# Four row groups at a time: low-rank pairs and head norms in the mixing stage of an RWKV-style block

## What is computed

```python
def token_shift_mix(z, mu):
    zp = jnp.pad(z, ((0, 0), (1, 1), (0, 0)))
    nb = 0.5 * (zp[:, :-2] + zp[:, 2:])
    return z + (nb - z) * mu

# in rwkv_branch
r, k, v = (token_shift_mix(z, mu[i]) for i, z in enumerate((r, k, v)))
uw, ua, ugt = (token_shift_mix(u, mu[i]) for i in (3, 4, 5))
g = jax.nn.sigmoid(ugt @ g1) @ g2                       # rank 96
kk = heads(k * k_k)
kk = kk / jnp.maximum(jnp.sqrt(jnp.sum(kk * kk, axis=-1, keepdims=True)), 1e-12)
for d in range(2):                                       # two directions
    logw = -softplus(-(w0[d] + jnp.tanh(uw @ w1[d]) @ w2[d])) - 0.5   # rank 32
    a = jax.nn.sigmoid(a0[d] + (ua @ a1[d]) @ a2[d])                  # rank 32
    k_d = k * (1.0 + (a - 1.0) * k_a)
bonus = jnp.sum(r_h * (k_dirs[0] + k_dirs[1]) * r_k, axis=-1, keepdims=True) * v_h
```

## Time and profile before

| | |
|---|---|
| median of 3 runs | 4121.08 us (4117.56 to 4122.92) |
| the profiled execution's own time | 4119.39 us |
| its span | 4117.3 us, 67491 instructions |
| busy: PE, DVE, ACT | 3582.8, 1924.8, 1135.2 us |
| mixing stage in the span | about 1016.6 to 1173.9 us |
| mean granted clock of TensorE | 0.946 |

### The profile page before, as it was taken

One profiled execution on the slowest core, in us unless ns is written; L12 is line 12 of the kernel. 1 busy time (PEld: TensorE's weight loads), 2 busy tenths in 40 slices (PEclk: granted clock), 3 DMA queues, 4 the chain that ended last, 5 costly groups with the idle time before them and its releaser, 6 DMA issues. The chain is left out here.

```text
span 4117.3 us, 67491 instructions
## 1 busy us (share of the span) xinstructions
PE 3582.8 (87%) x30260; PEld 2871.7 (70%) x30260; DVE 1924.8 (47%) x2773; ACT 1135.2 (28%) x1702; POOL 75.9 (2%) x85
## 2 busy tenths in 40 slices
PE   1999799998757777769999999989778899999998
PEld 1888677886236666737888888767556668888885
DVE  6565456543755565545322222467785462222225
ACT  2211221013523443323211111235464331111113
POOL 0000000000000000000000000020000020000000
PEclk9999899999769999979999999999889999999999
DMA  4233311222652122132111111211000111111112
GB/s 171 90 102 117 120 57 46 87 92 90 234 175 65 45 70 75 44 127 82 45 51 47 51 47 52 62 53 41 6 1 1 62 51 52 46 52 47 51 43 91
DMA packets 146015, 292.25 MB, mean 71 GB/s; under 512 B 8592, under 2 KB 83856, under 8 KB 145472
## 3 DMA queue, kind: packets, MB, share of 16 engines
q1 hardware_dynamic: 124672, 233.73, 18.2%
q10 hardware_dynamic: 21056, 54.22, 3.5%
HBM read 234.67 MB, written 52.99 MB: 70 GB/s over the span
## 5 line engine op out<-in xcount | busy, mean ns | idle before, releaser
L303 DVE TENSOR_TENSOR ffn_wl<-ffn_raw,ffn_wh 128x1024 fp32r<-128x1024 f32 (+1 forms) x152 | 177.5, 1169 | 1017.6 <-ACT ffn_wh L300 1017.6
L335 PE MATMUL PS<-ffn_x_high,ffn_wh 128*128 128x512 f32 x1408 | 550.2, 391 | 15.5 <-DVE ffn_x_low L303 9.0
L336 PE MATMUL PS<-ffn_x_low,ffn_wh 128*128 128x512 f32 x1408 | 549.3, 390 | 0.0
L337 PE MATMUL PS<-ffn_x_high,ffn_wl 128*128 128x512 f32 x1408 | 549.1, 390 | 0.0
L300 ACT ACTIVATE ffn_wh<-ffn_raw 128x1024 fp32r<-128x1024 f32 (+1 forms) x152 | 153.8, 1014 | 1061.9 <-PE PS L337 1057.9
L335 PEld LDWEIGHTS PS<-ffn_x_high,ffn_wh 128*128 128x128 f32 x1408 | 265.1, 188 | 74.5 <-issue 12.5
L337 PEld LDWEIGHTS PS<-ffn_x_high,ffn_wl 128*128 128x128 f32 x1408 | 265.2, 188 | 55.3
L336 PEld LDWEIGHTS PS<-ffn_x_low,ffn_wh 128*128 128x128 f32 x1408 | 265.2, 188 | 54.8
L335 PE MATMUL PS<-ffn_hid_high,ffn_wh 128*128 128x512 f32 x704 | 276.0, 392 | 2.6 <-DVE ffn_wl L303 2.6
L337 PE MATMUL PS<-ffn_hid_high,ffn_wl 128*128 128x512 f32 x704 | 273.9, 389 | 0.0
L336 PE MATMUL PS<-ffn_hid_low,ffn_wh 128*128 128x512 f32 x704 | 273.9, 389 | 0.0
(11 more groups left out here) (416 smaller groups left out, 6404.6 us busy)
## 6 DMA issues: line engine op xcount, KB each, us to landing
ffn_raw<-in_ffn_up SPq DMA_DIRECT2D x88, 512.0 KB, 3.5
norm_e_t<-in_ada SPq DMA_DIRECT2D x32, 512.0 KB, 4.3
in_o_raw<-in_in_o SPq DMA_DIRECT2D x32, 512.0 KB, 3.5
ffn_raw<-in_ffn_down SPq DMA_DIRECT2D x32, 512.0 KB, 3.5
scan_tin<-scan_in SPq DMA_DIRECT2D x10, 1536.0 KB, 10.2
scan_in<-um ACTq DMA_DIRECT2D x20, 641.0 KB, 5.1
in_e_raw<-in_in_e SPq DMA_DIRECT2D x24, 512.0 KB, 3.6
ffn_raw<-in_ffn_down SPq DMA_DIRECT2D x32, 384.0 KB, 3.2
```

What stands on the lines that cost most here:

```text
L303: return nc.vector.tensor_tensor(out, x, high.bitcast(fp32), ALU.subtract)
L335: nc.tensor.matmul(out, wh, xh, start=k == 0, stop=False)
L336: nc.tensor.matmul(out, wh, xl, start=False, stop=False)
L337: last = nc.tensor.matmul(out, wl, xh, start=False, stop=k == kt - 1)
```

## The change

The pairs run over j, then c, then n. So two consecutive pairs are of n = 0 and n = 1 and read four different groups of 32 partitions of `hid`. The places in the block at which ACT and PE do something else are renumbered: on ACT `keep` of the r and v tiles stands behind the pair 1 (it was 2), `rest` of the next ones behind pair 3 (4) and `keep_bonus(j - 1)` behind pair 5 (4); on PE `bonus_sums(j - 1)` stands behind pair 3 and the second gate (behind pair 2). The stores of `lout` rows stand behind the pairs with c = 2, which are now the last two.

`nrm` and the two head matrices have 72 partitions or columns in place of 8 (`COPIES`): the eight head rows stand at 0, 32 and 64. The spread takes chunk c from the copy at 32 c.

```diff
+            COPIES = 64 + NH
-                nrm = sb(ctx, "kk_norm", [NH, PAD_T])
+                nrm = sb(ctx, "kk_norm", [COPIES, PAD_T])
-                heads_in = sb(ctx, "heads_in", [P, JB, NH])
-                heads_out = sb(ctx, "heads_out", [NH, JB, P])
+                heads_in = sb(ctx, "heads_in", [P, JB, COPIES])
+                heads_out = sb(ctx, "heads_out", [COPIES, JB, P])
-                pairs = [(j, n, c) for j in range(JB) for n in range(2) for c in range(3)]
+                pairs = [(j, n, c) for j in range(JB) for c in range(3) for n in range(2)]
...
 # ACT
                                 pair(i)
-                                if i % 6 == 2:
+                                if i % 6 == 1:
                                     for q in (2 * JB + 2 * j, 2 * JB + 2 * j + 1):
                                         keep(q)
-                                if i % 6 == 4 and j:
+                                if i % 6 == 5 and j:
                                     keep_bonus(j - 1)
-                                if i % 6 == 4 and j + 1 < JB:
+                                if i % 6 == 3 and j + 1 < JB:
                                     for q in (2 * JB + 2 * j + 2, 2 * JB + 2 * j + 3):
                                         rest(q)
...
 # PE, spread
-                                last = nc.tensor.matmul(PS[:, 4 * 512 + t:4 * 512 + t + w], heads_out[:, j, :],
-                                                        nrm[:, t:t + w], start=True, stop=True)
+                                at = slice(32 * c, 32 * c + NH)
+                                last = nc.tensor.matmul(PS[:, 4 * 512 + t:4 * 512 + t + w], heads_out[at, j, :],
+                                                        nrm[at, t:t + w], start=True, stop=True)
...
 # PE, main loop
                                 if i % 6 == 1:
                                     gate(j, 0)
-                                if i % 6 == 2 and j:
-                                    bonus_sums(j - 1)
                                 if i % 6 == 3:
                                     gate(j, 1)
+                                    if j:
+                                        bonus_sums(j - 1)
```

More of the change, by code:

```diff
@@ L1035, in _ @@
                             if q == 0:
-                                for x, name in ((low1, "low1"), (low1_g, "low1_g"), (heads_in, "heads_in"),
-                                                (heads_out, "heads_out")):
+                                for x, name in ((low1, "low1"), (low1_g, "low1_g"), (heads_in, "heads_in_3"),
+                                                (heads_out, "heads_out_3")):
                                     sp.dma_start(x[:, :, :], A[name]).then_inc(loaded.h, 16)
@@ L1112, in _ @@
                         act.wait_ge(M["kk_summed"], JB)
-                        nc.scalar.activation(nrm[:, :], PS[0:NH, 4 * 512:4 * 512 + PAD_T], ACT.Sqrt)\
+                        nc.scalar.activation(nrm[:, :], PS[0:COPIES, 4 * 512:4 * 512 + PAD_T], ACT.Sqrt)\
                             .then_inc(M["kk_root"], 1)
@@ L1246, in _ @@
                             for c, (t, w) in enumerate(PAD_CHUNKS):
-                                last = nc.tensor.matmul(PS[0:NH, 4 * 512 + t:4 * 512 + t + w], heads_in[:, j, :],
+                                last = nc.tensor.matmul(PS[0:COPIES, 4 * 512 + t:4 * 512 + t + w], heads_in[:, j, :],
                                                         sq[:, t:t + w], start=j == 0, stop=j == JB - 1,
@@ L3071, in constants @@
         heads[i, j, 2 * j + i // 64] = 1
+    heads_3 = np.zeros((P, JB, 64 + 2 * JB))
+    for at in (0, 32, 64):
+        heads_3[:, :, at:at + 2 * JB] = heads
     reset = np.ones((P, JB, P))
@@ L3091, in constants @@
             "heads_in": f(heads), "heads_out": f(heads.transpose(2, 1, 0)),
+            "heads_in_3": f(heads_3), "heads_out_3": f(heads_3.transpose(2, 1, 0)),
             "neg": f(np.where(before, NEG, 0.0)), "reset": f(reset), "masks": f(np.stack(masks, axis=1)),
```

## The result

| | before | with the change |
|---|---|---|
| median | 4117.56 us (5 runs, 4114.53 to 4122.92) | 4144.39 us (5 runs, 4134.74 to 4147.28) |
| ratio | | 1.0063, 95% interval 1.0052 to 1.0074 |
| profiled execution, span | 4119.39, 4117.3 | 4145.14, 4143.1 |
| mixing stage, first DVE instruction to the barrier's release | 1016.62 to 1174.10: 157.5 | 1017.17 to 1201.04: 183.9 |

The kernel became slower by 0.6%, 27 us. The stage grew by 26.4 us and the span by 25.8, so the whole loss lies in the stage. The forecast was 4150.5, the range 4136 to 4158.

A forecast was written before the change was run, and what follows sets the result against it. It took a chain over all engines, not PE or DMA load, to bound the loop. Terms 11.3 + 11.0 + 9.9 - 2.9 + 0.7 + 0.2 gave +30.2 us on 4119.4; forecast 4150.5, range 4136 to 4158.

The forecast's parts named there:

- The chain: Mixing stage, second half: each block is a chain over all engines from one `bonus` to the next, 21.4 us in block 1.
- three places: Where PE's load counts in the block: the gate, the bonus sums and the spread.
- The landing of five stores: ACT's queue behind `bonus_rows`: five stores of 3.08 MB land in order, the bonus store last, about 9.6 us after first issue.
- From landing to ACT's start 0.74: Between the bonus store's landing and ACT's first part of the next bonus: 0.74 us, part of the 15.1.
- The step for block 0: Block 0: `rest` falls into ACT's idle time, pairs 4 and 5 run together; `bonus(0)` starts earlier, -2.9 us.
- the 0.7 and 0.2 for larger head matrices: Loads: larger head matrices ahead of the second u tile, +0.7 us; wider weight loads of the head sums, +0.2 us.
- 2.08 for the spread: Spread on PE: three chunks beside each other cost about 2.1 us in place of 4.6, saving 0 to 2.5.
- the faster clock as a rival for gate and sums: PE granted 2.4 GHz: gate and sums cost 1.0 and 1.9 us less in each of three blocks, 4142; chance 13%.
- PE's packing carries: Rival at the 4.79 us wait for the spread: store lands within the spread's time, 2.5 saved per block, 4109; chance 4%.
- The store isn't held by its neighbours: Rival on the bonus store: it lands 5.2 us after the first issue, each block 4.4 shorter, 4137; chance 9%.
- The row groups do overlap: Answers the rival that row groups don't overlap: spread stays 4.6 us, only block 0 suffers, 4151 to 4152; chance 4%.
- The signs: Expected in the new profile: blocks of 32 and 30 us, late bonus store, waits on ACT of 10 us and more.

The follow-up runs named there:

- copies-only kernel: Kernel before with only the three copies of the norms and the spread over three row groups; 4113.0 against 4116.87 us, ratio 0.9992, repeated 0.9995.
- kernel with both moves back: Changed kernel with the bonus store issued right behind `bonus_rows` and the bonus sums ahead of the second gate; 4114.65 us against 4116.87 before, ratio 0.9996.
- the early start: Kernel with the first part behind pair 3, plus block 0's pairs ahead of the second gate, first r/v stores and gate store earlier; 4106.34 us, ratio 0.9976.
- kernel with the first part behind pair 3: Changed kernel with two bonus buffers, mixes in DVE's waits, sums, gates, spread and bonus's first part earlier; against kernel before ratio 1.0, repeated 0.9986.
- store first: Changed kernel with the bonus store issued as soon as `bonus_rows` is done, sums left behind the second gate; 4126.85 us against 4116.87 before, ratio 1.0023.

## Why the prediction was right

**The chain.** It said that the loop is a chain, that PE's load counts only at three places in it, and that the moved store would hold the next block. The four runs on this agree: one moved issue returned 5 to 6 us a block, one moved group of matmuls 3 to 4, both together all of it, and a second buffer, which takes away only the wait for the landing, 4 to 6.

**The sizes, term by term.** `bonus_rows` came 16.0 + 1.2 = 17.3 after `bonus` (17.6 forecast). From there to the next `bonus` it took 14.5 in block 1 (15.1). Block 1 lost 10.3 (11.3 forecast), block 2 9.6 (11.0), block 3 9.2 (9.9). Behind `bonus(3)` the stage was 0.3 shorter, which the sum left out. In all it is 29.1 in the blocks, less 2.0 for block 0, 0.4 for what is ahead of it and 0.3 for the end: 26.4 in place of 30.2. That is inside the range, but nearly 4 us less, as nearly every term had been taken too large. The landing of five stores, the largest term, was forecast as 9.6 after the first issue and measured as 9.7, 9.2 and 10.4. Block 3 has some luck in it: its first store was issued at T + 17.4 in place of 18.3, and the landing took 0.8 longer than forecast, so that it came at T + 27.8 (27.9 forecast).

**One term was wrong in kind.** "From landing to ACT's start 0.74" was read from the kernel before, where the store landed at 1118.25 and ACT began at 1118.99. But ACT was issuing two other stores until 1118.88, in a row of the kernel before that the earlier trace rows leave out:

```profile
1118.07 0.81 ACTq L1094 DMA_DIRECT2D scan_in<-um  x2
```

ACT began 0.11 after the end of these issues. In block 2 of the same kernel, where ACT had nothing left to issue, the store landed at 1140.55 and ACT began at 1140.62; with the change it begins 0.02 after the landing. This makes 0.7 in each block: all that the forecast had too much behind `bonus_rows` in block 1, 0.7 of 1.1 in block 2, and all of the 0.7 in block 3.

**Issues were taken as equal.** The step for block 0 has "0.84, 0.81, 0.84, 0.81". The second pair of issues took 1.61 (a store of the series in the earlier trace rows that took 1.27 had shown it), so block 0, from DVE's clamp of the norms to `bonus(0)`, shrank by 2.0, from 20.4 to 18.5, and not by 2.9.

**The loads.** Of the 0.7 and 0.2 for larger head matrices, DVE's wait for the second u tile rose from 0.23 to 0.43, and each head sum from 2.32 to 2.37; the clamp came 61.4 after the stage's start in place of 61.9. The 0.9 were not paid: the first head sum took 3.73 in place of 4.43, at a mean granted clock of 0.62 in that stretch in place of 0.50. What raised the clock there was not tested.

**The clock.** The forecast took 2.08 for the spread; it took 1.13, at a granted clock of 1.00 (the second of the stage windows above). In the copies-only kernel the same spread took 2.08 at 0.50. Where I had kept the faster clock as a rival for gate and sums, these took 2.08 and 3.62 in block 1, as at 0.50 (2.08 and 3.78 before), and the clock rose only behind them. The spread is off the chain: in time it gave little.

**The rivals.** "PE's packing carries" named a real saving, 2.5 us of wait per block, and the copies-only kernel shows what the spread's packing is worth by itself, the kernel with both moves back what it is worth with the pairs': less than can be measured. "The store isn't held by its neighbours" falls with the landings. The row groups do overlap.

**The signs.** The bonus store came 6.9 behind `bonus_rows`, and the spread's first pass started at 1114.45, with three under way by 1114.55. DVE waited 11.6 and 11.2 for ACT's first part in blocks 1 and 2, but 9.2 in block 3, not 10. Its wait for the spread was 1.33 and not 2.3, by the clock. The DMA share was 0.73 in block 1, where under 0.7 was forecast, and 0.58 in block 2.

## What to carry to other kernels

A place in an engine's order is worth more than the work on it: a store whose landing the next iteration waits for belongs right behind the instruction that makes its data, ahead of everything that could run later, and a matmul that the loop waits for doesn't belong behind one that is released late. Before packing an engine's work denser, find which of its waits anyone stands in; busy 93% did not say so here. And when the order is mended, look at what idles next: here it was the DMA queue under an 8 us reciprocal. With it started early the second half was 7.6 to 10 us shorter in the profiles than in the same kernel without that. The time shows a gain of 9 to 10 us over the kernel before; what the early start has of it the noise hides.

## What the runs showed of the hardware

- A float32 matmul with a contraction of 32 rows overlaps with three others on other groups of 32 partitions: eight passes of two 512-column pairs took 1.99 us in the kernel before (same two groups twice) and 1.14 with the change (four groups), both at the start of block 0 and at a granted clock of 1.00. Three groups in the spread took 2.08 at 0.50 (copies only), where the same passes in one group took 4.6.
- Copying eight rows to three places costs nothing on the engines that make them: root, clamp and reciprocal on 72 partitions took 1.24, 0.82 and 8.16 us, on 8 partitions 1.23, 0.81 and 8.15.
- Issuing a DMA on ACT took 0.33 to 0.45 us for the first three of a quick series of 641 KB stores and, with the change, about 1.2 us for the fourth of these and the bonus store behind it; the fourth took 0.6 in blocks 1 and 2 of the kernel with the first part behind pair 3. That time is ACT's, and I had not expected it. It isn't the number of stores not yet landed: in the kernel with the first part behind pair 3 a bonus store issued at 1125.4, 7 us behind the one before it and with stores in the queue that landed up to 1136, took 0.33. Beyond that the cause stays open.
- TensorE's granted clock was 1.00 at the spread of block 1 with the change, where it was 0.50 in the kernel before. A less busy PE is not the whole of it: in the kernel before, PE was busy without a pause from 1119.0 to 1128.4 at 0.50, and the clock then rose to a mean of 0.81 from 1128.4 to 1133.9, the second gate taking 1.12. What raises it was not tested.
- A 512 KB store issued 6.7 us behind the one before it landed after 2.6 us (store first, block 1), which the prediction had estimated as 2.65. With the change, behind four stores of 641 KB, it landed 9.2 to 10.4 us after the first of them was issued. In the kernel before it took 4.7 and 6.7 in blocks 1 and 2. There the v tile's store, issued some 4 us ahead of it (1108.8 and 1130.1), was still in flight and landed 7.0 to 7.9 after its own issue. The prediction laid the 4.7 to loads; no run tells the two apart.
